# Rotary swap by a VectorE shuffle on paired columns, two PSUM banks for transposes alone, and attention's weight products in parts of three spread over the tiles

## The reference

```python
rq_h = rotary(split_heads(rq, RET_HEADS), pos) * (HEAD_DIM ** -0.5)
rk_h = rotary(split_heads(rk, RET_HEADS), pos)
ret = bidirectional_retention(rq_h, rk_h, ...)
pool = multiscale_pool(pv, pool_w, pool_scale)
na = merge_heads(neighbourhood_attention(...))
mo = merge_heads(memory_attention(...))
up = jnp.einsum('bsnc,ncd->bsnd', branches, w_branch)
gates = jax.nn.sigmoid(h @ w_gate).reshape(b, s, N_BRANCH, dm)
x = x + jnp.einsum('bsnd,bsnd->bsd', gates, up) @ w_out
a, g = jnp.split(rms_norm(x, norm_ffn_g) @ w_ffn_in, 2, axis=-1)
return x + (jax.nn.silu(a) * g) @ w_ffn_out
```

```python
t1, t2 = tf[..., :half], tf[..., half:]
return jnp.concatenate([t1 * cos - t2 * sin, t1 * sin + t2 * cos], axis=-1)
```

## Time and profile before

| | us |
|---|---|
| median of 3 runs | 3743.36 |
| lowest, highest | 3739.09, 3751.61 |
| span of the profiled execution (its own time: the page gives no other) | 3740.9 |
| TensorE busy | 3376.3 (90%) |
| VectorE, ScalarE, GpSimd busy | 1683.3 (45%), 766.3 (20%), 1828.4 (49%) |

### The profile page before, as it was taken

The page is one execution under the profiler, slowest core; times in us unless marked ns, Lnnn a source line. Parts: engine busy times, 40 slices in busy tenths (PEclk is TensorE's granted clock), DMA queues, the critical chain, the costliest instruction groups (busy, mean ns, idle before and its releaser), DMA issues.

```text
span 3740.9 us, 45117 instructions
## 1 busy us (share of the span) xinstructions
PE 3376.3 (90%) x14188; PEld 2569.3 (69%) x14188; DVE 1683.3 (45%) x2422; ACT 766.3 (20%) x1562; POOL 1828.4 (49%) x1020
## 2 busy tenths in 40 slices
PE   4888999999878989998897978989998999989998
PEld 3554787888655468787785555768886666768886
DVE  5445336322555352453426444763226544653224
ACT  3321112100233211110102334231002233231001
POOL 4123565666532166665565120736666322446664
PEclk7788999999978799999998688989999999899999
DMA  3011223222221022222222010212222111222222
GB/s 139 29 40 54 83 96 106 96 96 96 84 74 34 28 85 96 93 96 80 89 91 74 23 59 12 99 62 96 96 97 94 47 46 40 73 71 94 98 99 85
DMA packets 78350, 285.00 MB, mean 76 GB/s; under 512 B 8688, under 2 KB 9200, under 8 KB 77424
## 3 DMA queue, kind: packets, MB, share of 16 engines
q1 hardware_dynamic: 74736, 269.41, 21.2%
q10 hardware_dynamic: 3456, 13.50, 1.0%
HBM read 280.78 MB, written 2.10 MB: 76 GB/s over the span
## 4 chain that ended last, share of the span: by engine, by line
PE 74%; DVE 17%; ACT 4%; issue 3%; DVEq 1%; DMA 0%; ACTq 0%; SPq 0%
PE pa L488 34%; PE pd L488 30%; PE po L649 3%; PE pd L630 3%; DVE work L167 2%; DVE qs L167 2%; DVE b_lo L167 2%; PE pa L638 1%; DVE h_lo L167 1%; ACT work L163 1%; PE po L682 1%; PE pd L668 1%; DVE pair L167 1%; DVE work L171 1%; DVE work L187 1%
## 5 line engine op out<-in xcount | busy, mean ns | idle before, releaser
L443 POOL TENSOR_SCALAR w_hi<-w_raw 128x1024 fp32r<-128x1024 f32 x508 | 552.4, 1087 | 1840.0 <-PE pa L488 1162.8
L445 POOL TENSOR_TENSOR w_lo<-w_raw,w_hi 128x1024 fp32r<-128x1024 f32 x508 | 1276.7, 2513 | 42.4
L488 PE MATMUL pa<-h_hi,w_hi 128*128 128x512 f32 x1888 | 770.4, 408 | 56.7 <-issue 52.9
L488 PE MATMUL pa<-h_lo,w_hi 128*128 128x512 f32 x1888 | 754.0, 399 | 0.0
L488 PE MATMUL pa<-h_hi,w_lo 128*128 128x512 f32 x1888 | 751.8, 398 | 0.0
L488 PE MATMUL pd<-b_hi,w_hi 128*128 128x512 f32 x1152 | 464.0, 403 | 68.5 <-DVE x_res L167 45.5
L488 PEld LDWEIGHTS pa<-h_hi,w_hi 128*128 128x128 f32 x1888 | 366.9, 194 | 166.6 <-issue 77.8
L488 PE MATMUL pd<-b_lo,w_hi 128*128 128x512 f32 x1152 | 457.2, 397 | 0.0
L488 PE MATMUL pd<-b_hi,w_lo 128*128 128x512 f32 x1152 | 456.5, 396 | 0.0
L488 PEld LDWEIGHTS pa<-h_hi,w_lo 128*128 128x128 f32 x1888 | 365.9, 194 | 79.4
L488 PEld LDWEIGHTS pa<-h_lo,w_hi 128*128 128x128 f32 x1888 | 366.6, 194 | 78.1 <-issue 3.0
(11 more groups left out here) (153 smaller groups left out, 3558.1 us busy)
## 6 DMA issues: line engine op xcount, KB each, us to landing
w_raw<-in_w SPq DMA_DIRECT2D x508, 512.0 KB, 3.2
mrg<-in_mem ACTq DMA_DIRECT2D x4, 1024.0 KB, 4.8
mrg<-in_nabias ACTq DMA_DIRECT2D x2, 2048.0 KB, 9.0
x_res<-in_x SPq DMA_DIRECT2D x8, 256.0 KB, 5.2
out_y<-mrg ACTq DMA_DIRECT2D x8, 256.0 KB, 2.1
mrg<-in_count ACTq DMA_DIRECT2D x2, 512.0 KB, 3.5
kbuf<-in_delta ACTq DMA_DIRECT2D x2, 448.0 KB, 7.9
rope<-in_rope SPq DMA_DIRECT2D x1, 512.0 KB, 11.6
```

Of the source, the lines that this page charges most:

```text
L443: nc.gpsimd.tensor_scalar(w_hi[:, j], raw[:, j % RR], 1.0, 1.0, ALU.mult, ALU.mult).then_inc(rounded, 1)
L445: nc.gpsimd.tensor_tensor(w_lo[:, j], raw[:, j % RR], w_hi[:, j].bitcast(F32), ALU.subtract)\
L488: ins = mm(out, a, b, start=(first and k == 0 and e == 0), stop=(last and k == k_n - 1 and e == 2))
```

## The change

The swap matmuls are gone. The columns of the weights of rotary products are paired: GpSimd's split of these 29 chunks (`PAIRED`) writes column i of a half next to column i of the other half, and the rotary table and its frequencies are loaded in the same order, so that the swap is an exchange of neighbours within 32 partitions, `stream_shuffle` with NEXT (or with SWAP, an exchange of 16 and 16, for latent attention, whose columns stay as they were). The pa ring has two banks and a new ring tr has two for the T transposes. `schedule` cuts each linear among the pieces into parts of three matmuls and puts out, behind each N, as many parts as keep them even over all tiles of the pair. The memory's norm sum becomes nine pieces of its own. `pool_mix` does two gates, the pool's matmuls, and then the other two gates.

```diff
@@ -73,7 +76,19 @@
-CREDIT = {"pa_done": RA, "pd_done": RD, "sq_used": 2, "acc_part": 2, "qk_full": 2, "e_full": 0, "pv_done": 2}
+def paired_chunks():
+
+    block1, even, _ = chunk_counts()
+    ret = {l * block1 + 12 + 4 * p + k for l in range(2) for p in range(2) for k in range(2)}
+    swa = {2 * block1 + k for k in (0, 2, 3, 4, 5)}
+    dil = {2 * block1 + even + 3 * p + k for p in range(8) for k in range(2)}
+    return ret | swa | dil
+
+
+PAIRED = paired_chunks()
+
+
+CREDIT = {"pa_done": RA, "tr_done": RT, "pd_done": RD, "sq_used": 2, "acc_part": 2, "qk_full": 2, "e_full": 0, "pv_done": 2}
...
@@ -287,8 +310,11 @@
+
+PARTS = {"Cq": KT, "Ck": KT, "Cv": KT, "Cg": KT, "Cm0": 3, "Cm1": 3, "Cm2": 2, "L0": KT, "L1": KT, "L2": KT, "L3": KT, "L4": KT}
+
...
@@ -299,16 +325,15 @@
-
-                at = {2: (1, 4), 3: (1, 4, 6)}.get(len(todo), range(1, n)) if n == 8 else range(1, n)
+                todo = [(what, to, k, PARTS.get(what, 1)) for what, to in todo for k in range(PARTS.get(what, 1))]
+                size = len(todo)
         for what, behind in (("N", 1), ("T", 2), ("O", 3)):
...
                 yield (what, *divmod(s - behind, n))
-            if what == "N" and s < total and todo and a in at:
-                yield ("piece", *todo.pop(0))
-        if s < total and a == n - 1:
-            for one in todo:
-                yield ("piece", *one)
+            if what == "N" and s < total:
+                left = size - size * (a + 1) // n
+                while len(todo) > left:
+                    yield ("part", *todo.pop(0))
...
@@ -434,22 +471,33 @@
         def _(pool):
-            def split(i, j, first):
+            def split(i, j, first, paired=False):
                 pool.wait_ge(loaded[j % RR], (i * (RW // RR) + j // RR + 1) * 16)
...
                 pool.sem_inc(turn, 1)
-                nc.gpsimd.tensor_scalar(w_hi[:, j], raw[:, j % RR], 1.0, 1.0, ALU.mult, ALU.mult).then_inc(rounded, 1)
+                src, hi, lo = raw[:, j % RR], w_hi[:, j], w_lo[:, j]
+                if paired:
+                    src = src.rearrange("p (h f i) -> p h i f", f=2, i=32)
+                    hi, lo = (w.rearrange("p (h i f) -> p h i f", f=2, i=32) for w in (hi, lo))
+                nc.gpsimd.tensor_scalar(hi, src, 1.0, 1.0, ALU.mult, ALU.mult).then_inc(rounded, 1)
                 pool.wait_ge(rounded, i * RW + j + 1)
-                nc.gpsimd.tensor_tensor(w_lo[:, j], raw[:, j % RR], w_hi[:, j].bitcast(F32), ALU.subtract)\
-                    .then_inc(wsplit, 1)
-
-            for j in range(RW):
-                split(0, j, True)
-            with pool.Fori(1, NCHUNK // RW) as i:
-                for j in range(RW):
-                    split(i, j, False)
+                nc.gpsimd.tensor_tensor(lo, src, hi.bitcast(F32), ALU.subtract).then_inc(wsplit, 1)
+
+            c = 0
+            while c < NCHUNK:
+                run = 0
+                while c % RW == 0 and c >= RW and c + run < NCHUNK and not PAIRED & set(range(c + run, c + run + RW)):
+                    run += RW
+                if run > RW:
+                    with pool.Fori(c // RW, (c + run) // RW) as i:
+                        for j in range(RW):
+                            split(i, j, False)
+                    c += run
+                else:
+                    split(c // RW, c % RW, c < RW, c in PAIRED)
+                    c += 1
...
@@ -543,35 +599,44 @@
-            def rot(mat):
-                i = n.take("qk_full")
-                bank = bank_d()
-                pe.wait_ge(pa_done, n.at("pa_done", n.qs_item[i % 2]))
-                n.take("pd_full")
-                mm(bank[:, :], mat, qs[:, i % 2], start=True, stop=True).then_inc(pd_full, 1)
-
-            n.qs_item = [0, 0]
-            n.qs_n = 0
-
-            def note_qs():
-                n.qs_item[n.qs_n % 2] = n.n["pa_done"] - 1
-                n.qs_n += 1
+            def in_parts(bank, src=H, k_n=KT, k_0=0, slot=None, w_0=0):
+
+                s = next_chunk() if slot is None else slot
+                assert not n.norm_ends
+                for k in range(k_n):
+                    ins = products(bank[:, :], [w_tile(s, w_0 + k)], [act_tile(src, k_0 + k)], k == 0, k == k_n - 1)
+                    if k < k_n - 1:
+                        yield
+                return ins
             def piece(ph, p, what):
-                if what in ("Cq", "Ck"):
+
+                if what in ("Cq", "Ck", "Cv", "Cg") and n.norm_ends:
                     linear(bank_a()).then_inc(cdone, 1)
-                    if ph.kind != "cross":
-                        note_qs()
-                    if ph.kind in ("na", "mem", "cross"):
-                        n.take("late")
-                elif what == "Cv":
-
-                    linear(bank_a()).then_inc(cdone, 1)
+                    noted(ph, what)
+                else:
+                    for _ in parts(ph, p, what):
+                        pass
+
+            def noted(ph, what):
+                if what == "Cv":
                     n.vt_item = n.take("late")
-                elif what == "M":
-                    memory_root()
+                elif what == "Cg" or what in LATENTS.pieces() or (what in ("Cq", "Ck") and ph.kind in ("na", "mem", "cross")):
+                    n.take("late")
+
+            def parts(ph, p, what):
+                if what in ("Cq", "Ck", "Cv", "Cg") or what in LATENTS.pieces():
+                    ins = yield from in_parts(bank_a())
+                    ins.then_inc(cdone, 1)
+                    noted(ph, what)
+                elif what in SUMS:
+                    if what == "M0":
+                        n.sum_bank = bank_a()
+                    else:
+                        k = int(what[1]) - 1
+                        add_square(n.sum_bank, k, KT, ones, MEM)
                 elif what in ("Rq", "Rk", "Rq2"):
-                    rot(swap96 if ph.kind == "mla" else swap64)
+                    n.take("qk_full")
                 elif what in ("Nq", "Nk"):
...
@@ -605,9 +668,13 @@
                 base = {}
-                for what, p, a in schedule(ph, after):
-                    if what == "piece":
-                        piece(*a, p)
+                work_on = None
+                for what, p, a, *part in schedule(ph, after):
+                    if what == "part":
+                        if part[0] == 0:
+                            work_on = parts(*a, p)
+                        done = next(work_on, "done")
+                        assert (done == "done") == (part[0] == part[1] - 1), (a, p, part)
                         continue
...
@@ -631,19 +698,19 @@
                         g = n.take("tile_t")
-                        bank = bank_a()
-                        base[p, a] = n.n["pa_done"] - 1
+                        bank = bank_t()
+                        base[p, a] = n.n["tr_done"] - 1
                         pe.wait_ge(n_full, n.at("n_full", g))
...
                             ins = nc.tensor.transpose(bank[:, k * P:k * P + P], pr[:, g % 3, k * P:k * P + P], ident)
-                        n.take("pa_full")
-                        ins.then_inc(pa_full, 1)
+                        n.take("tr_full")
+                        ins.then_inc(tr_full, 1)
                     elif what == "O":
...
                             pe.wait_ge(*n.po_release[p % 2])
-                        pe.wait_ge(pa_done, n.at("pa_done", base[p, a]))
+                        pe.wait_ge(tr_done, n.at("tr_done", base[p, a]))
                         for k in range(kn):
...
@@ -703,6 +770,7 @@
                     ins.then_inc(pd_full, 1)
+                some_gates(2)
                 for m in range(2):
...
@@ -1455,12 +1531,9 @@
                 dve.wait_ge(pa_done, n.at("pa_done", i_qs))
-                v.tensor_tensor(pair2[:, 0], qs[:, q % 2], rope[:, tables], ALU.mult).then_inc(dc, 1)
-                c = n.at("dc", n.take("dc"))
-                i = full_d(False)
-                v.tensor_tensor(pair2[:, 1], pd[i % RD][:, :], rope[:, tables + 1], ALU.mult).then_inc(pd_done, 1)
-                dve.wait_ge(dc, c)
-                dve.wait_ge(pd_done, n.at("pd_done", i))
+                chain(v.tensor_tensor(pair2[:, 0], qs[:, q % 2], rope[:, tables], ALU.mult))
+                chain(v.stream_shuffle(pair2[:, 1], qs[:, q % 2], SWAP if tables else NEXT))
+                chain(v.tensor_tensor(pair2[:, 1], pair2[:, 1], rope[:, tables + 1], ALU.mult))
                 if not with_root:
...
```

More of the change, by code:

```diff
@@ L31 @@
 DELTA = S + MAX_REACH
+NEXT = [i ^ 1 for i in range(32)]
+SWAP = [i ^ 16 for i in range(32)]
 EPS = 1e-6
@@ L510, in _, with add_square @@
             n.norm_ends = None
+            def add_square(bank, k, k_n, mat, width):
+                i = n.take("sq_used")
+                pe.wait_ge(sq_full, n.at("sq_full", i))
+                mm(bank[:, 0:width], mat, sq[:, i % 2, 0:width], start=(k == 0), stop=(k == k_n - 1))\
+                    .then_inc(sq_used, 1)
```

(23 more changed lines are left out.)

105 lines of the change are left out of this document (61 added, 44 removed).

## The result

The changed kernel takes 3817.53 us (median of 4 runs, 3809.26 to 3819.03) against 3744.37 for the kernel before: ratio 1.0191, 95% interval 1.0174 to 1.0207: some 71 us slower by the ratio, 73 by the medians. The forecast was slower too, but by 29 us (3772), in a range that ended at 3798.

What follows compares the result with a forecast made beforehand. TensorE's work, at its granted clock, plus its waits was taken as the bound. Terms 18 + 10 - 4 - 3 - 4 - 10 + 22 = 29 us on 3743.4 gave 3772 us, range 3710 to 3798.

Steps and rivals of the forecast that it cites:

- the hybrid layers: Memory, neighbourhood attention, retention and pool together: -5 us a layer, twice, so -10.
- the dilated stage: Seven dilated pairs going from 36.9 to 39.5 us, +2.6 per pair, +18 in all.
- the rotary part: Rope: 38 swaps of 1.0 us leave TensorE; VectorE's chain grows 0.8 us, hidden in mid-pair, paid where the next pair waits.
- Ends: Late parts make Tv and the next scores wait: +5.4 us per dilated, +7.7 per latent, +6.3 per sliding pair.
- Sliding window: Three pairs going from 29.3 to 28.2 us, with 4.3 of clock gained: -3; the last pair -4.
- Latent attention: Three pairs going from 27.4 to 30.8 us: +10; the last pair -4.
- Rings: Two pa banks: 7.9 us of idle and +11 in each cross attention, +4 in each hybrid memory stage.
- the order of the gates: Pool in each hybrid layer: the wait of 7.78 us grows, that of 4.62 goes, +3.5.
- The spread: Parts over all tiles cover TensorE's idle time: 2.6 us per dilated, 4.3 per latent, 3 per sliding pair.
- The clock did not stay up: Rival: spread parts keep TensorE at 2.4 GHz through the attention, 57 us of clock gained, 3715 us; chance 0.27.
- The rings' waits were not hidden: Rival: the bank waits in cross attention and hybrid layers are hidden, so 22 and 8 us go, 3743 to 3750; chance 0.14.
- GpSimd's paired split: Reordering taken as costing nothing; by the skill's rule half as much again, 5.5 us; slow-reordering rival 3780 us, chance 0.06.

Runs made afterwards that it cites:

- swap_unread: Kernel before with the rope by shuffle on paired columns, the swap matmuls still made, unread but waited for; 3789.47 us, ratio 1.0121.
- shuffle_only: Kernel before with only the rope by shuffle and paired columns; four pa banks, whole pieces, four gates first; 3780.99 us, ratio 1.0107.
- extra_step: Kernel before with one more shuffle in each rope's VectorE chain, its result overwritten, swaps kept and read; 3771.49 us, ratio 1.0078.
- early: Changed kernel with parts over tiles 0 to 5 (latent 0 to 2), key's rope at 6, value's transposes at 7; 3766.71 us, ratio 1.0083.
- gates22: Kernel before with only the pool's order changed: two gates, the pool's matmuls, two gates; 3741.51 us, ratio 0.9996.
- whole_pieces: Changed kernel without the spread: whole linears at single tiles, rings, shuffle and gate order as changed; 3827.46 us, ratio 1.0231.

## Why the prediction was wrong

The direction held, and so did the waits at the pairs' ends and for the ring's bank; the sum was short by 42 us. By the stages' table it was short in the sliding pairs by 21 us, in the hybrid layers by 15 and in the dilated stage by 15, and it was too high by 11 in the two cross attentions. That last error hid part of the others.

**The step that failed** is the rotary part: "2.0 us per dilated pair (two swaps)", and with it "the chain grows by 0.8 us, hidden where the rope is made in mid-pair". The sum took off 27 us for swaps (7 x 2.0, 3 x 1.0, 3 x 2.1, 2 x 2), and charged the added step only at the pairs' ends. swap_unread beside shuffle_only shows the 38 swaps to be worth 5 us, at most 17, and nothing in the dilated pairs, where their absence let the clock fall; extra_step, whose ropes stand where the kernel before has them, shows that the step held hidden costs 28, in the dilated pairs mostly by the clock again (13.1 of 16.8 us). The shuffle by itself, forecast as a gain, costs 40. In extra_step's trace the added step was hidden as expected in the sliding pairs and the hybrid layers, and not in the dilated and latent pairs.

**Ends.** Place and order were right: Tv waits 2.04 and the next score 3.3 to 4.2 at the dilated ends, and the score 6.2 to 6.9 at sliding and 7.2 to 7.5 at latent ones. The dilated pairs are 40.7 us long (3226.61 - 2982.50 over 6, the first scores), forecast 39.5:

```profile
2982.50 0.79 PE L697 MATMUL pd<-kbuf,qbuf 64*128 64x128 f32 x2 [4.22 <-DVE kbuf L182]
...
3226.61 0.79 PE L697 MATMUL pd<-kbuf,qbuf 64*128 64x128 f32 x2 [3.38 <-DVE kbuf L182]
```

**Sliding window.** Forecast 28.2 with 4.3 of clock gained; the first scores of the changed kernel start 33.2, 29.2 and 33.5 apart (the third, at 2116.13, is shown above), and the clock was 0.76:

```profile
2053.72 0.79 PE L697 MATMUL pd<-kbuf,qbuf 64*128 64x128 f32 x2 [6.17 <-DVE qbuf L182]
...
2086.94 0.79 PE L697 MATMUL pd<-kbuf,qbuf 64*128 64x128 f32 x2 [6.92 <-DVE qbuf L182]
...
2149.59 0.79 PE L697 MATMUL pd<-kbuf,qbuf 64*128 64x128 f32 x2 [6.93 <-DVE qbuf L182]
```

This term had the wrong sign. The pair of 29.2 is the one whose later scores are back at the upper clock, 0.70 us for what takes 1.22 in the others (2097.36 and on); that the gap of 7 us at each end is what undoes the spread's gain is my reading, supported by early, where the sliding pairs are 9 us shorter than before.

**Latent attention.** Forecast 30.8 a pair. The waits of 7.2 to 7.5 us at the ends came as expected, but the pairs are 25.3 and 28.5 us from first score to first score, together as long as the same two before (53.8 against 53.6), so the spread took off more between them than the sum had.

**Rings.** Predicted as 7.9 us of idle and +11 in each cross attention; the wait is 10.05, but the stages grew by 6 and 4. In the hybrid memory stages the wait was 8 us where I had +4, and in the pool 6 per layer, where I had put +3.5 down to the order of the gates, which costs nothing (gates22). The price of rings and gates together, 46 us between whole_pieces and shuffle_only, is above my 37, within its interval of 14; its place was not as forecast, 33 in the hybrid layers where I had 15.

**The spread.** It covers idle time as forecast (L705's wait 21.5 against 50.7) and is worth some 15 us; placed early, 40 more.

**The rivals.** The clock did not stay up; its deciding mark, the first part after a pair's end, takes 1.58 us at the sliding ends (2116.92 in the chain), which is the lower clock. The rings' waits were not hidden. GpSimd's paired split, on average over the 29, takes 1.27 + 2.79 us, where the other 479 take 1.08 + 2.51. One of them, beside the earlier trace rows:

```profile
3056.32 1.25 POOL L484 TENSOR_SCALAR w_hi<-w_raw 128x1024 fp32r<-128x1024 f32 x1 [8.40 <-issue]
3057.66 2.92 POOL L486 TENSOR_TENSOR w_lo<-w_raw,w_hi 128x1024 fp32r<-128x1024 f32 x1
```

That is an eighth more, not half. The rule that the prediction cites from the Trainium skill ("GPSIMD Engine Reference", Performance pitfalls for Q7 kernels) did not show at that size; for these two operations the measurement decides. What the longer splits cost the steps beside them may be part of the 16 us that stay open.

## What to carry to other kernels

Work taken off the busiest engine saved next to nothing here, since that engine then ran at a lower clock between another engine's steps; ask first, for each instance, what ends last there, and read the granted clock beside the busy time. A step put on the chain that TensorE waits for can cost more than its own length when the wait it makes lets TensorE's clock fall, and its price is then seen in the matmuls behind, not at the wait. When parts of a product are spread to the very end of a stage, what hangs on its result, and the transfers and splits that its end releases, all land together in front of the next stage.

## What the runs showed that was not expected

Unread matmuls can make a kernel faster: a kernel slowed by a VectorE step got back 12 of 28 us with 24 of them, and they took the kernel before to 0.9977, of which almost half came elsewhere. A shuffle of 128x512 takes 0.73 us with either of the two patterns (726 ns mean over 38, 720 to 736), preceded by a mask load of 0.01. The rope's second product no longer reads PSUM and has two SBUF operands; its mean is 759 ns against 692, and the three of its 38 that took over 1 us lay beside GpSimd's splits.
